# Compress's second weight in four pieces, and the second unit's products in plain order

## The reference

```python
def compress_rows(rows, pe, w1, w2):
    ...
    chunks = rows.reshape(B, nch, CMP_STRIDE, NSA_GROUPS, NSA_DK)      # CMP_STRIDE = 16 tokens
    w1r = w1.reshape(R, CMP_STRIDE, NSA_DK, CMP_HID)                   # R = 2, CMP_HID = 256
    nc = nch - R + 1
    h = jnp.einsum('ld,ldh->h', pe, w1.reshape(CMP_BLOCK, NSA_DK, CMP_HID))
    for r in range(R):
        part = jnp.einsum('bcjgd,jdh->bcgh', chunks, w1r[r])
        h = h + part[:, r:r + nc]
    return jnp.einsum('bcgh,hd->bcgd', jax.nn.gelu(h), w2)
```

## Time and profile before

| what | value |
|---|---|
| median of 3 runs | 1606.74 us (1606.26 to 1613.9) |
| the profiled execution's own time | 1612.34 us |
| its span, first to last instruction | 1610.5 us |
| TensorE busy over the span | 1513.5 us (94%) |
| VectorE busy | 849.6 us (53%) |
| ScalarE busy | 604.1 us (38%) |
| mean granted TensorE clock | 0.971 |

### The profile page before, as it was taken

One profiled execution on the slowest core, in us unless ns is written; L12 is line 12 of the kernel. 1 busy time (PEld: TensorE's weight loads), 2 busy tenths in 40 slices (PEclk: granted clock), 3 DMA queues, 4 the chain that ended last, 5 costly groups with the idle time before them and its releaser, 6 DMA issues. The chain is left out here.

```text
span 1610.5 us, 31774 instructions
## 1 busy us (share of the span) xinstructions
PE 1513.5 (94%) x12648; PEld 1262.9 (78%) x12648; DVE 849.6 (53%) x1814; ACT 604.1 (38%) x1165; POOL 186.6 (12%) x269
## 2 busy tenths in 40 slices
PE   8999999999899978898887988999899999999998
PEld 5888888877799966665555757676679999999998
DVE  4866533214798748777785534545454432244322
ACT  5322211314454437666764323333433321133210
POOL 1000000000544100083421000000000000000000
PEclk9999999999899999999998989989899999999999
DMA  7635468544333275334422999998624334343321
GB/s 209 200 121 175 152 248 297 187 104 98 85 110 112 60 199 160 72 131 125 144 80 81 371 363 361 364 335 306 238 67 130 106 112 123 104 130 117 92 78 56
DMA packets 186010, 265.79 MB, mean 165 GB/s; under 512 B 36381, under 2 KB 117725, under 8 KB 185766
## 3 DMA queue, kind: packets, MB, share of 16 engines
q1 hardware_dynamic: 174930, 227.27, 43.3%
q0 software_dynamic: 6016, 25.34, 5.3%
q10 hardware_dynamic: 4948, 11.62, 2.0%
HBM read 241.11 MB, written 42.60 MB: 176 GB/s over the span
## 5 line engine op out<-in xcount | busy, mean ns | idle before, releaser
L751 PE MATMUL pj_ps<-all_hi,pj_xh 128*128 128x512 f32 x480 | 192.0, 400 | 0.2 <-DVE all_lo L623 0.2
L753 PE MATMUL pj_ps<-all_hi,pj_xl 128*128 128x512 f32 x480 | 189.9, 396 | 0.0
L752 PE MATMUL pj_ps<-all_lo,pj_xh 128*128 128x512 f32 x480 | 189.8, 395 | 0.0
L3178 PE MATMUL fi_ps<-fi_th,fi_wh 128*128 128x272 f32 x512 | 147.6, 288 | 1.7 <-DVE fi_tl L2935 1.7
L3179 PE MATMUL fi_ps<-fi_fl,fi_wh 128*128 128x272 f32 x512 | 148.5, 290 | 0.0
L3180 PE MATMUL fi_ps<-fi_th,fi_wl 128*128 128x272 f32 x512 | 148.3, 290 | 0.0
L3178 PE MATMUL fi_ps<-fi_fh,fi_wh 128*128 128x272 f32 x512 | 147.8, 289 | 0.0
L3180 PE MATMUL fi_ps<-fi_fh,fi_wl 128*128 128x272 f32 x512 | 147.6, 288 | 0.0
L3179 PE MATMUL fi_ps<-fi_tl,fi_wh 128*128 128x272 f32 x512 | 147.2, 287 | 0.0
L2493 ACT ACTIVATE de_slot<-de_ps_t 128x512 f32<-128x512 f32 (+5 forms) x124 | 62.8, 513 | 176.9 <-PE de_ps_t L2327 92.6
L2603 DVE COPY de_slot<-de_ps_t 128x512 f32<-128x512 f32 (+4 forms) x112 | 68.7, 622 | 111.4 <-PE de_ps_t L2327 66.5
(11 more groups left out here) (406 smaller groups left out, 3325.1 us busy)
## 6 DMA issues: line engine op xcount, KB each, us to landing
de_dv<-in_cache_diff SPq DMA_DIRECT2D x64, 512.0 KB, 9.9
all_big<-in_w_in SPq DMA_DIRECT2D x14, 2048.0 KB, 9.7
de_dk<-in_cache_diff SPq DMA_DIRECT2D x48, 512.0 KB, 9.9
all_big<-in_cache_nsa SPq DMA_DIRECT2D x64, 256.0 KB, 6.4
all_big<-in_w_up SPq DMA_DIRECT2D x16, 1024.0 KB, 5.6
all_big<-in_w_down SPq DMA_DIRECT2D x16, 1024.0 KB, 5.6
all_dk<-in_cache_diff SPq DMA_DIRECT2D x16, 512.0 KB, 8.0
all_win<-in_cache_win SPq DMA_DIRECT2D x32, 256.0 KB, 7.5
```

The costliest lines, as they stand in the source:

```text
L751: pe.matmul(ps[:, t, :], xh[:, k, xk], wh[:, u, k, :], start=k == 0, stop=False)
L752: pe.matmul(ps[:, t, :], xh[:, k, xk], wl[:, u, k, :], start=False, stop=False)
L753: return pe.matmul(ps[:, t, :], xl[:, k, xk], wh[:, u, k, :], start=False, stop=k == KT - 1)
L3178: pe.matmul(o, hi[:, k, :], a_hi[:, k, tok], start=k == 0, stop=False)
```

## The change

The second weight's steps are cut in four pieces y = 0 to 3, piece y for quarter y. A piece of the split is rows 2y and 2y+1 of both halves (`quarter_of`, 128x2x512), a piece of the sum and of its split is 128x512. On ScalarE split pieces come at w = 1 to 4 and the sum's at w = 3 to 6, on VectorE at w = 2 to 5 (split and add) and w = 4 to 7 (split of the sum). In unit 1 TensorE waits for piece q ahead of quarter q, and the quarters' products and sums alternate as in the other units.

```diff
+        quarter_of = lambda x, y: x.rearrange("p (h j) n -> p h j n", h=2)[:, :, 2 * y:2 * y + 2, :]
...
-            def split():
+            def split(y):
                 act.wait_ge(w1_in[1], 16 * 8)
-                nc.scalar.activation(w1h[1], raw_w1[1], ACT.Copy).then_inc(w1_hi, 1)
+                nc.scalar.activation(quarter_of(w1h[1], y), quarter_of(raw_w1[1], y), ACT.Copy).then_inc(w1_hi, 1)
-            def split_sum(k):
-                act.wait_ge(w_sum, k + 1)
-                nc.scalar.activation(wsh[k], first_w1[k], ACT.Copy).then_inc(w_sum_hi, 1)
+            def split_sum(y):
+                act.wait_ge(w_sum, y + 2)
+                nc.scalar.activation(wsh[1][:, 2 * y:2 * y + 2, :], first_w1[1][:, 2 * y:2 * y + 2, :], ACT.Copy).then_inc(w_sum_hi, 1)
...
-                if w == 1:
-                    split()
-                if w == 3:
-                    split_sum(1)
+                if w <= QUARTERS:
+                    split(w - 1)
+                if 3 <= w < 3 + QUARTERS:
+                    split_sum(w - 3)
...
+            def split(y):
+                dve.wait_ge(w1_hi, y + 2)
...
+            def sum_weights(y):
+                rows = slice(2 * y, 2 * y + 2)
+                dve.wait_ge(w1_lo, y + 2)
+                dve.wait_ge(pe_mm, 2)
...
+            def split_sum(y):
+                rows = slice(2 * y, 2 * y + 2)
+                dve.wait_ge(w_sum_hi, y + 2)
...
-                if w == 2:
-                    split()
+                if 2 <= w < 2 + QUARTERS:
+                    split(w - 2)
                 if w == 3:
                     position_sums()
-                    sum_weights(1)
-                if w == 4:
-                    split_sum(1)
+                if 2 <= w < 2 + QUARTERS:
+                    sum_weights(w - 2)
+                if 4 <= w < 4 + QUARTERS:
+                    split_sum(w - 4)
...
-                    pe.wait_ge(w1_lo, 2)
                     pe.wait_ge(pe_ready, 1)
+                if n == 1:
+                    pe.wait_ge(w1_lo, q + 2)
...
-                if q == 0 and n < 2:
-                    pe.wait_ge(w_sum_lo, n + 1)
+                if n == 0:
+                    pe.wait_ge(w_sum_lo, 1)
+                if n == 1:
+                    pe.wait_ge(w_sum_lo, q + 2)
...
-                ahead = RING if n == 1 else 0
-                for q in range(ahead):
-                    chunks(n, q)
                 for q in range(QUARTERS):
                     if q == 3 and n:
                         second(n - 1)
                     if (n, q) == (0, 3):
                         position_columns()
-                    if q >= ahead:
-                        chunks(n, q)
+                    chunks(n, q)
                     chunk_sums(n, q)
```

More of the change, by code:

```diff
@@ L1055, in position_sums @@
                 nc.vector.tensor_copy(pe_h[:], ph[:, 5, COLS:COLS + 4]).then_inc(pe_ready, 1)
[L1057 to L1069, removed]
+            def split(y):
+                dve.wait_ge(w1_hi, y + 2)
+                nc.vector.tensor_tensor(quarter_of(w1l[1], y), quarter_of(raw_w1[1], y), quarter_of(w1h[1], y).bitcast(F32),
+                                        ALU.subtract).then_inc(w1_lo, 1)
+            def sum_weights(y):
+                rows = slice(2 * y, 2 * y + 2)
+                dve.wait_ge(w1_lo, y + 2)
+                dve.wait_ge(pe_mm, 2)
+                nc.vector.tensor_tensor(first_w1[1][:, rows, :], first_w1[1][:, rows, :], second_w1[1][:, rows, :], ALU.add
+                                        ).then_inc(w_sum, 1)
+            def split_sum(y):
+                rows = slice(2 * y, 2 * y + 2)
+                dve.wait_ge(w_sum_hi, y + 2)
+                nc.vector.tensor_tensor(wsl[1][:, rows, :], first_w1[1][:, rows, :], wsh[1][:, rows, :].bitcast(F32),
+                                        ALU.subtract).then_inc(w_sum_lo, 1)
             def lay_out(w):
```

## The result

| | before | changed |
|---|---|---|
| median, all of one comparison | 1608.67 us (5 runs, 1606.26 to 1613.9) | 1597.27 us (5 runs, 1596.61 to 1597.97) |
| ratio to before, 95% interval | | 0.9926 [0.9903, 0.9950] |
| span of the profiled execution | 1610.5 us | 1595.4 us |
| mean granted TensorE clock | 0.971 | 0.975 |
| first product of unit 0 to the prompt's first product | 171.4 us | 162.0 us |

The account below looks back on a forecast made before the run. TensorE was taken as the bound (busy 94%), with the gather chain limiting the gain: 1.5 + 3.2 less 0.3 gives 4.4 us, so 1606.74 becomes 1602.3 us; range 1597.5 to 1607.5.

Parts of the forecast that it names:

- Units 0 and 1 on TensorE: TensorE's compression timeline: fewer waits and less slow running were to let unit 2 start 8.9 us earlier.
- the replay: Step-by-step timing of VectorE, ScalarE and TensorE in units 0 and 1 from measured operation prices; unit 2 8.9 us earlier.
- the slow stretch that the range made room for: TensorE at half clock behind a wait in unit 1: some 3.4 us long, 1.7 us lost, not charged in the forecast.
- The first gather's 4.96 us: GpSimd, pair 1: VectorE's long weight split held this gather; with pieces it takes 1.8 us, 3.2 saved.
- The chain of gathers: Layout of quarter 4, four gather slots, layouts of 11 and 12, next pair: no slack; it was to gain 4.4 us.
- The other 15 gathers: GpSimd, pair 1, all gathers after the first: they meet short VectorE operations as before, so their gain was set at nothing.
- layout of 11: VectorE's layout of quarter 11, which needs pair 1's last gather landed; forecast at about 444.4 instead of 448.82.
- moves as a whole: Everything behind the layout of quarter 11, including pair 2's gathers, was to shift by the same amount, with no further gain.
- the new wait: VectorE at the layout of quarter 11, idle 3.5 us for gathers because it would arrive at about 441.
- 4.5 given back in unit 2: TensorE in unit 2 waits on data held up by the gathers, losing 4.5 of the 8.9 us gained.
- the gathers do not bind and the 8.9 us stay whole: Rival: GpSimd's gathers do not limit the compression, so the full gain stays, 1597.8 us; chance 0.12.
- The sum: Whole kernel: 4.4 us off the median of 1606.74 us, 1602.3 us; everything behind the compression moves equally.

Follow-up runs that it names:

- a_again: The changed kernel unaltered, run and profiled a second time; median 1597.89 us, ratio 0.9947 to the kernel before.
- block_pieces: The kernel before with VectorE's 128x4096 subtraction of the second weight cut into four 128x1024 ones in the same place; 1607.16 us in one run.
- late_gather: The changed kernel, with pair 1's first gather also waiting for VectorE's low part of quarter 3; median 1601.28 us, ratio 0.9974 to the kernel before.
- whole_plain: The kernel before with only TensorE's plain order of products and sums in unit 1, the weight left whole; median 1608.56 us, ratio 1.0014.
- b_again: The kernel before unaltered, run and profiled a second time; median 1607.66 us, ratio 1.0004.
- a_noland: The changed kernel without GpSimd's wait for one slot's landing before issuing the next slot's gathers; median 1592.03 us, ratio 0.9914 to the kernel before.

## Why the prediction was wrong

**What was right.**
- Units 0 and 1 on TensorE: unit 2 could start 8.9 us earlier by the replay; 8.4 were measured in the first pair of profiles and 5.5 in the second, where the clock fell differently. There were three waits of 0.3, 1.1 and 1.9 us. The clock stayed up in the changed kernel's first profile; in `a_again` it was 0.53 in 430 to 432, behind the third wait, so the slow stretch that the range made room for does come.
- The first gather's 4.96 us were the weight's split: 1.75 after, and 1.76 in `block_pieces`, where nothing else changed. The section of the Trainium skill that was weighed there (SBUF — State Buffer, Who interferes with whom, Practical consequences) has its rule for two SBUF inputs right by these runs as far as VectorE comes first. Its inference, that tensor_tensor leaves descriptor generation alone, does not carry over to these gathers, which read their row numbers (`all_row_ids`) from SBUF: both rows end 0.8 us behind the subtraction.
- The chain of gathers limits what an earlier unit is worth: `late_gather` loses 3.4 us of the median by 4.2 us at its head, and in `whole_plain` the whole gain is given back in a wait of 4.80 us.

**The step that failed.** "The other 15 gathers meet short operations as before, some 128x512 pieces more and two long ones (1.96 and 1.90) fewer, which I set at nothing." They gained 2.5 us, 1.55 of it in the first slot, whose three others went from 1.43, 1.43 and 1.96 to 1.02, 0.94 and 1.31. The rows for a better value were there: the two long ones, 1.96 and 1.90 against 0.95 undisturbed, are up to 2.0 us. With them the chain would have gained 6.4 of the 6.7 measured at layout of 11.

**A second step, of the same size.** "What goes on from there (layout of 12, pair 2's gathers, 491.31) moves as a whole". It did not: from layout of 11 to that of 27 the gain grew by 2.5 us in both pairs of profiles, 1.7 and 1.8 of it in pair 2 and 0.8 and 0.7 in pair 3, where the second weight has long been done. In pair 2 the sixteen gathers took 19.2 and 19.4 us before and 17.7 and 18.8 after, and the three waits for landings between them 10.0 and 11.7 against 9.9 and 10.5; in pair 3 the gathers took the same and the waits 10.6 and 10.5 against 9.7 and 9.8. Correcting the first step alone, 1606.74 - 6.7 = 1600.0 us, would still have been 2.8 us too high.

**What hung on it.** With layout of 11 at 442.56 instead of 444.4 (444.8 with this execution's later start), and VectorE there 0.8 us later than the replay had it, the new wait shrank from 3.5 to 0.34 us. So the "4.5 given back in unit 2" did not come: unit 2 started 8.4 us earlier, and the units as a whole ended 9.4 us earlier in the first profile, 8.8 in the mean of two. The rival "the gathers do not bind and the 8.9 us stay whole" gave the time within 0.5 us, but that was luck, since its reason is wrong: the gathers do bind at layouts 19 and 27 (4.86 us of waiting at each), and up to layout of 11 they were shortened by about as much as VectorE was.

**The sum.** It was set against 1606.74 us, the median of three executions, of a kernel whose executions spread over 15 us. Its other medians are 1606.1 to 1608.7, so the starting point was uncertain by about 2 us. The units ended 9.4 us earlier where the sum has 4.4, and the median is 9.5 us below 1606.74, so the miss of 5.0 us lies in the compression: 2.3 us up to layout of 11, 2.5 behind it.

**Open.** Why the same code behind the compression takes 1029.6 to 1040.9 us from one profile to the next; and why pairs 2 and 3 go 1.7 and 0.8 us faster in the changed kernel. The gain showed in both pairs of profiles, but in pair 2 one kernel's own two profiles differ by as much (42.5 and 44.3, 40.8 and 42.6), and no run here separates the two.

## What to carry to other kernels

Where a GpSimd gather is on a critical chain, read for each gather which VectorE operation runs when it starts, and price all of them, not only the longest: cutting long two-input operations speeds up the gathers too. A reordering on the bounding engine is worth nothing while another chain ends at the same point; free both (here the order: nothing with the chain and the weight whole, some 4 us without the chain), and count a gain off both. When executions of one kernel spread over 15 us, a profile of each kernel may differ by 6 us in code that neither changed; compare stretches between fixed points, in more than one profile, and medians of many runs.

## What was not expected of the hardware

- Gathers that start within a VectorE operation with both inputs in SBUF, at least 0.15 us before its end, end 0.80 to 0.84 us behind it. This holds for 322 gathers of pairs 1 to 3 in the timelines of the twelve profiles, behind operations from 128x512 (0.65 us) to 128x4096 (4.41 us); the seven that start within 0.04 us of the operation's own start were not held. The 79 that start during a transpose and the 40 that start during an operation with one input in PSUM (`cm_pc`, `cm_ph`) take the undisturbed 0.94 or 0.95.
- The other way round nothing is held: 90 VectorE subtractions and additions that started while an undisturbed gather was running took the same 0.65 to 0.69 and 1.21 to 1.23 us as elsewhere.
- The same waits may or may not bring the clock down: a wait of 2.04 us was followed by 0.50 in the first profile of before, and the same wait, 2.04 us, by full speed in `b_again`.
- Sixteen gathers without waits for landings between the slots worked at one every 1.4 us on the average (22.3 us for 16), and the landings kept up: no layout waited for one in `a_noland`.
